# Second block: the gate projection in the last three rounds of the recurrent stage, its sigmoids from copies

## The chip, the cores and the metric

The kernel runs on one core of a Trainium2 chip. The metric is the device time of one execution in microseconds, the median of three runs. Everything is 32-bit floating point.

## The reference

Two transformer blocks run one after the other on 512 tokens of width 1024. The change is in the second. There one input projection feeds two branches, a gated delta rule (eight heads of 128, forwards and backwards over chunks of 64 tokens) and latent attention. A sigmoid gate for each branch weighs their outputs:

```python
h = rms_norm_2(x, g_mix[l]) * (1.0 + sc1) + sh1
proj = h @ w_in[l]
dn_qkv, dn_z, dn_b, dn_a, c_q, c_kv, k_r, gates = jnp.split(proj, split_at, axis=-1)
y_dn = gated_deltanet_branch(dn_qkv, dn_z, dn_b, dn_a, ...) @ w_o_dn[l]
y_mla = mla_branch(c_q, c_kv, k_r, ...) @ w_o_mla[l]
g_dn, g_mla = jnp.split(jax.nn.sigmoid(gates), N_BRANCHES, axis=-1)
merged = g_dn * y_dn + g_mla * y_mla
x = x + gt1 * (merged @ w_out[l])
```

After it come the router and sixteen experts. The part of `proj` that the change moves is `g_dn`'s, columns 4960 to 5983 of `w_in`, called `gd` in the kernel.

## The kernel before

Activations lie transposed: 128 channels on the partitions, 512 tokens along them, eight such tiles (`h3` for `h`). A projection of width 1024 is eight products j, each of eight matmuls (kk) of 128x128 weights by 128x512 into one PSUM bank. In the trace each 32-bit matmul has two records, so a projection to 1024 has 128.

The code writes out one instruction list for each engine, as Python generators. `woven` (L96) takes one step of each stream in turn, and such a step is a **slot**. `rounds` (L1244) starts 12 rounds of 32 slots. In round r the recurrent ("delta") stage runs five stages on different heads: the fetch of head r (its projections), the preparation of r-1, the scores of r-2 (the triangular inverse, many 64x64 products), the state chain of r-3, and the post stage of r-4. In a slot their order is chain, scores, post, preparation, fetch, and after these what is given as `beside`. Round 8 has no fetch left, round 9 only chain 6, scores 7 and post 5, round 10 chain 7 and post 6, round 11 post 7. Each queue is carried out in order, so a wait holds all that stands behind it.

**The chain** (`pe_dchain` L2432, `ac_dchain` L2472) has eight steps of four slots: in slot 0 products with the state, in slot 1 the one of the inverse (after ScalarE has scaled the last), in slot 2 two more (after ScalarE's copy U2), and nothing in slot 3. VectorE then updates the state for the next step. The end of the last step of head 7 is marked `dheaded 7`. **The post stage** (`pe_dpost` L2522, `ac_dpost` L2545) turns a head's output with 32 short products in slot 1 and sums squares with one 128x512 product in slot 6; ScalarE takes a logarithm and an exponential in slot 8, for heads over 4 with a table load ahead of them. `pe_dscores` (L2301) issues nothing in slots that are 3 (mod 4), but for one group in slot 3.

**The latent stage** follows (`pe_mla` L2668, `ac_mla` L2699, `sp_mla` L2644, `dv_mla` L2731). `gd` is its first projection (L2669), into banks 3 and 4, each bank emptied by a sigmoid into `ga3` (L2704). Then come cq (four products, banks 2 and 1), a wait for cq's last copy, ck (two products), kr (one), and the output projection `odn` of the delta branch. `odn` waits for all the `gd` sigmoids (L2683), since VectorE multiplies each of its products by `ga3` (L2752). After `odn`'s second product TensorE does the rotation of kr and sums the squares of cq and ck, which ScalarE has made after kr's copy, a sine and a cosine and a table load.

**Loads.** SP issues all weight loads in one order. `Ring` has five slots of 1 MB; `claim` (L272) waits for TensorE to have freed what a slot held. `sp_mla` begins with a wait for `dheaded 7` and the load of the positions; the loads of `gd` stand behind it (L2647).

Of the kernel before, what the change touches and what calls it, by code (L numbers as in the profile page):

```python
# [104 lines left out]
def run(stream):  # L105
    for _ in stream:
        pass


def chain(*streams):  # L110
    for s in streams:
        yield from s


def idle(n):
# [96 lines left out]
def program(nc, a, out):  # L212

    ctx = ExitStack()
    with ctx:
# [1028 lines left out]
        def rounds(*stages, beside={}):  # L1244

            for r in range(8 + len(stages) - 1):
                woven(*[stages[n](r - n) for n in (3, 2, 4, 1, 0) if 0 <= r - n < 8], *[beside[n]() for n in beside if n == r])
# [893 lines left out]
        def sp_dfetch(sp, hd):  # L2141
            src = [rows128(win[:, b0 + hd * 128:b0 + hd * 128 + 128]) for b0 in (0, 1024, 2048, 3072)]
            for i in range(2):
                load(sp, ("dq", hd, i), (0, (0, P), (8, 128), src[2 * i]), (1024, (0, P), (8, 128), src[2 * i + 1]))
# [441 lines left out]
        def none32(ct):  # L2586
            yield from idle(32)

        def sp_delta(sp):
            sp_gates(sp)  # L2590
            for hd in range(8):
                sp_dfetch(sp, hd)

        def pe_delta(pe):
            pe_gates(pe)
            nx = (s_dv, ndv["nx", "mix2", 0])
            left = {0: nx, 1: nx, 2: nx, 3: nx}
            rounds(lambda c: pe_dfetch(pe, c, left), lambda c: pe_dprep(pe, c, left), lambda c: pe_dscores(pe, c, left),
                   lambda c: pe_dchain(pe, c), lambda c: pe_dpost(pe, c, left))

        def ac_delta(ac):
            ac_gates(ac)
            rounds(lambda c: ac_dfetch(ac, c), lambda c: ac_dprep(ac, c), lambda c: ac_dscores(ac, c), lambda c: ac_dchain(ac, c), lambda c: ac_dpost(ac, c))

        def gp_delta(gp):
            gp_gates(gp)
# [37 lines left out]
        def sp_mla(sp):  # L2644
            sp.wait_ge(s_pe, npe["dheaded", 7])
            sp.dma(pi, a["pos"].broadcast_to([P, 512])).then_inc(s_pos, 16)
            run(sp_proj(sp, "gd", win[:, 4960:5984], KT, D))  # L2647
            run(sp_proj(sp, "cq", win[:, 4128:4640], KT, 512))
            run(sp_proj(sp, "ck", win[:, 4640:4896], KT, 256))
            k = claim(sp, ("kr",), 2)  # L2650
# [15 lines left out]


        def pe_mla(pe):  # L2668
            run(pe_proj(pe, "gd", h3, KT, D, (3, 4), lambda j: (s_ac, nac["gd", j])))  # L2669
            pe.wait_ge(s_dv, ndv["dof", 7])  # L2670
            run(pe_proj(pe, "cq", h3, KT, 512, (2, 1), lambda j: (s_ac, nac["cq", j])))
            pe.wait_ge(s_ac, nac["cq", 3])
            run(pe_proj(pe, "ck", h3, KT, 256, (2, 1), lambda j: (s_ac, nac["ck", j])))
            k, there = ring["kr",]
            v = wv(k, 0, (0, P), (8, 128))
# [4 lines left out]
            m.then_inc(s_pe, npe("kr"))  # L2680
            pe.wait_ge(s_dv, ndv["dpost", 7])
            odn = pe_proj(pe, "odn", od3, KT, D, (0, 1), lambda j: (s_dv, ndv["odn", j]))
            pe.wait_ge(s_ac, nac["gd", 7])  # L2683
            pe.wait_ge(s_ac, nac["ck", 1])
            for j, _ in enumerate(odn):
                if j == 1:
# [12 lines left out]
        def ac_mla(ac):  # L2699
            ac.wait_ge(s_pe, npe["dheaded", 7])  # L2700
            ac.wait_ge(s_dv, ndv["doo", 7, 7])
            for j in range(8):
                ac.wait_ge(s_pe, npe["pj", "gd", j])
                ac.act(ga3[:, j, :], BK[3 + j % 2][:, :], ACT.Sigmoid).then_inc(s_ac, nac("gd", j))  # L2704
            for key, src, nk, *_ in LATS:
                for j in range(nk):
                    ac.wait_ge(s_pe, npe["pj", key, j])
                    ac.act(src[:, j, :], BK[2 - j % 2][:, :], COPY).then_inc(s_ac, nac(key, j))
            ac.wait_ge(s_pe, npe["kr"])
            ac.wait_ge(s_dv, ndv["pos"])  # L2710
            ac.act(R0, BK[7][:, :], COPY).then_inc(s_ac, nac("rope", "kr"))
            ac.wait_ge(s_dv, ndv["ang"])
            ac.act(SI, ang, ACT.Sin).then_inc(s_ac, nac("sin"))
            ac.act(CO, ang, ACT.Sin, scale=0.5).then_inc(s_ac, nac("cos"))
# [893 lines left out]
```

## Time and profile before

| | us |
|---|---|
| median of three runs | 3571.12 |
| lowest, highest | 3561.42, 3572.17 |
| the profiled execution | 3565.9 |
| its span | 3564.1 |

| engine | busy us | share |
|---|---|---|
| TensorE, matmul | 3423.7 | 96% |
| TensorE, weight load | 2251.5 | 63% |
| VectorE | 1521.5 | 43% |
| ScalarE | 752.4 | 21% |
| GpSimd | 354.5 | 10% |

The times of the rows are from the start of the span. Matmuls are pipelined and their ends are modelled, so TensorE's busy time holds some overlap; the distance from one start to the next is the safer measure. "Idle before" in brackets is the time the engine stood idle ahead of the group, with what ended it. A line of the timeline merges like instructions. The rounds of the delta stage can be found by the 32 short products of the post stage (`con,A 64*128 64x64`): they start at 2322.78 for round 7, 2388.87 for round 8, 2436.34 for round 9, 2475.85 for round 10 and 2508.79 for round 11. The gate projection `gd` runs from 2516.42.

### The profile page before, as it was taken

The numbers are of one execution on the slowest core, as the hardware profiler recorded it, in microseconds if no ns is written. First come the engines' busy times: TensorE is split into PE (matmuls) and PEld (weight loads), VectorE is DVE, ScalarE is ACT, GpSimd is POOL, SyncE is SP. The second block draws the span as 40 slices with busy tenths as digits, with TensorE's granted clock in tenths as the row PEclk, the third lists the DMA queues.
The fourth block names the chain that finished last, engine by engine and source line by source line (L and its number), as shares of the span: only waits on it lengthen the run. The fifth ranks groups of instructions, "written<-read, shape, count | busy, mean of one in ns | idle before, by whom it ended". The sixth has DMA issues, their size and how long they took to land.

```text
span 3564.1 us, 56007 instructions
## 1 busy us (share of the span) xinstructions
PE 3423.7 (96%) x24870; PEld 2251.5 (63%) x24870; DVE 1521.5 (43%) x2761; ACT 752.4 (21%) x1564; POOL 354.5 (10%) x274
## 2 busy tenths in 40 slices
PE   8999998999999999999998999998999999899999
PEld 3566676888884658888885566566445656534344
DVE  4454454788743225778633444544112204201011
ACT  2323232211003035211002222233112320211111
POOL 0010110233000000122001110012000001000000
PEclk9999998999999999999999999999899999899999
DMA  5321202255641320256522101000321114599996
GB/s 195 119 73 45 85 7 84 86 174 179 207 146 48 84 71 1 60 177 198 157 73 71 48 25 37 2 2 2 103 65 42 48 43 148 241 421 421 421 421 256
DMA packets 355809, 453.12 MB, mean 127 GB/s; under 512 B 25712, under 2 KB 282992, under 8 KB 331760
## 3 DMA queue, kind: packets, MB, share of 16 engines
q1 hardware_dynamic: 355568, 449.55, 36.8%
q8 instruction: 195, 3.19, 0.4%
q14 instruction: 46, 0.38, 0.0%
HBM read 445.27 MB, written 4.20 MB: 126 GB/s over the span
## 4 chain that ended last, share of the span: by engine, by line
PE 90%; DVE 5%; ACT 3%; issue 1%; DMA 1%; SPq 0%; POOLq 0%; POOL 0%; DVEq 0%; ACTq 0%
PE bank L79 90%; DVE A L70 2%; DVE A L76 1%; ACT A L87 1%; ACT H L87 1%; PE bank L82 0%; DVE X L76 0%; DVE H L70 0%; ACT SM L87 0%; DVE SM L76 0%; DVE A L73 0%; DMA A<-in_x 0%; ACT L90 0%; ACT X L87 0%; DMA W<-in_mlp_up 0%
## 5 line engine op out<-in xcount | busy, mean ns | idle before, releaser
L79 PE MATMUL bank<-A 64*64 64x64 f32 (+4 forms) x13728 | 1078.6, 263 | 55.3 <-ACT A L87 35.1
L79 PEld LDWEIGHTS bank<-A 64*64 64x64 f32 (+2 forms) x13728 | 862.3, 150 | 295.5 <-issue 126.6
L79 PE MATMUL bank<-A,W 128*128 128x256 f32 (+1 forms) x2240 | 721.1, 476 | 3.0 <-DMA W<-in_rw_g 1.8
L79 PE MATMUL bank<-H,W 128*128 128x512 f32 (+2 forms) x1712 | 625.4, 519 | 17.0 <-ACT H L87 14.4
L79 PEld LDWEIGHTS bank<-A,W 128*128 128x128 f32 x2240 | 418.9, 191 | 254.3 <-issue 213.0
L87 ACT ACTIVATE A<-bank 128x512 f32<-128x512 f32 (+5 forms) x517 | 223.3, 435 | 1537.1 <-PE bank L79 1493.4
L79 PEld LDWEIGHTS bank<-H,W 128*128 128x128 f32 (+1 forms) x1712 | 316.6, 190 | 288.8 <-issue 258.8
L79 PE MATMUL bank<-A,H 128*64 128x512 f32 (+2 forms) x1224 | 310.5, 574 | 6.9 <-ACT H L87 6.4
L70 DVE TENSOR_TENSOR A<-bank,A 128x256 f32<-128x256 f32 (+1 forms) x350 | 157.5, 461 | 184.3 <-PE bank L79 164.3
L79 PEld LDWEIGHTS bank<-A,H 128*64 128x64 f32 (+1 forms) x1224 | 114.8, 146 | 173.1 <-issue 146.0
L70 POOL TENSOR_TENSOR A<-A 128x512 f32<-128x512 f32 (+1 forms) x103 | 146.4, 1428 | 739.0 <-ACT A L87 372.2
L87 ACT ACTIVATE A<-A 128x512 f32<-128x512 f32 (+1 forms) x230 | 133.8, 609 | 376.9 <-DVE A L70 358.4
L79 PE MATMUL bank<-W,H 128*64 128x512 f32 (+3 forms) x952 | 208.8, 475 | 4.8 <-ACT H L87 4.8
L76 DVE SCALAR_TENSOR_TENSOR SM<-W,cact,SM 128x512 f32<-128x512 f32 x206 | 184.4, 895 | 9.3
L70 DVE TENSOR_TENSOR A<-W 128x512 f32<-128x512 f32 x152 | 110.8, 770 | 177.7 <-PE bank L79 87.4
L70 DVE TENSOR_TENSOR A<-bank,SM 128x512 f32<-128x512 f32 x16 | 10.3, 686 | 392.9 <-PE bank L79 392.9
L79 PEld LDWEIGHTS bank<-W,H 128*64 128x64 f32 (+1 forms) x952 | 85.6, 159 | 104.2 <-issue 98.4
L70 POOL TENSOR_TENSOR SM<-SM 128x512 f32<-128x512 f32 x31 | 41.2, 1329 | 819.6 <-ACT SM L87 817.3
L79 PE MATMUL bank<-H,A 128*128 128x256 f32 x448 | 107.4, 381 | 0.0
L76 DVE SCALAR_TENSOR_TENSOR X<-bank,mods,X 128x256 f32<-128x256 f32 (+1 forms) x144 | 86.4, 602 | 48.5 <-PE bank L79 43.6
L79 PE MATMUL bank<-A,con 128*128 128x512 f32 (+2 forms) x174 | 91.5, 650 | 14.4 <-ACT A L87 14.4
L70 DVE TENSOR_TENSOR A<-A 128x512 f32<-128x512 f32 (+3 forms) x58 | 54.0, 940 | 102.3 <-ACT A L87 101.3
(179 smaller groups left out, 2551.1 us busy)
## 6 DMA issues: line engine op xcount, KB each, us to landing
A<-in_w_gate SPq DMA_DIRECT2D x47, 1024.0 KB, 19.3
W<-in_mod_w SPq DMA_DIRECT2D x45, 1024.0 KB, 7.3
A<-in_w_up SPq DMA_DIRECT2D x42, 1024.0 KB, 15.3
A<-in_w_down SPq DMA_DIRECT2D x35, 1024.0 KB, 25.4
W<-in_mlp_up SPq DMA_DIRECT2D x64, 512.0 KB, 5.4
W<-in_mlp_down SPq DMA_DIRECT2D x128, 256.0 KB, 4.0
W<-in_w_mod SPq DMA_DIRECT2D x24, 1024.0 KB, 5.6
W<-in_w_up SPq DMA_DIRECT2D x22, 1024.0 KB, 14.6
```

Of the source, the lines that this page charges most:

```text
L70: return self.e.tensor_tensor(o, x, y, op)
L76: return self.e.scalar_tensor_tensor(out=o, in0=x, scalar=s, in1=y, op0=op0, op1=op1, **kw)
L79: return self.e.matmul(o, l, r, start=start, stop=stop, skip_group_check=True)
L87: return self.e.activation(o, i, func, bias=bias, scale=scale)
```

## The change

`gd`'s 64 matmuls become a stream `pe_dgate` that is given to `rounds` as `beside` for rounds 9, 10 and 11, 32 steps of it in each (`take`). A product j takes nine slots: eight with one matmul each and an empty one, so it covers slots 9j to 9j+7 counted from the start of round 9, and the last matmul stands in slot 6 of round 11. All go into bank 0. In each ninth slot ScalarE copies the bank to one of eight free places `GDR`, and the next product waits for that. The four loads are issued at the end of `sp_delta`, ahead of the wait for `dheaded 7`. In the latent stage cq is now first and uses banks 3 and 4, the wait ahead of ck is on post 7's variance, and the eight sigmoids read the copies, after kr's copy and ahead of the sine.

```diff
@@ -110,6 +110,13 @@
 def chain(*streams):
     for s in streams:
         yield from s
+
+
+def take(stream, n):
+
+    for _ in range(n):
+        next(stream, None)
+        yield
 
 
 def idle(n):
@@ -2586,21 +2593,54 @@
         def none32(ct):
             yield from idle(32)
 
+
+
+        GDR = [A[:, k:k + 512] for k in (26624, 27136, 27648, 28160, 21184, 21696, 22208, 22720)]
+
+        def pe_dgate(pe):
+            pe.wait_ge(s_ac, nac["r1"])
+            for j in range(8):
+                lk = ("pj", "gd", j // 2 * 256)
+                k, there = ring[lk]
+                pe.wait_ge(ring.sems[k], there)
+                if j:
+                    pe.wait_ge(s_ac, nac["gdr", j - 1])
+                for kk in range(8):
+                    m = pe.mm(BK[0][:, :], wv(k, 0, (0, P), (8, 256))[:, kk, j % 2 * 128:j % 2 * 128 + 128], h3[:, kk, :], kk == 0, kk == 7)
+                    if kk < 7:
+                        yield
+                if j % 2:
+                    npe.mark_next("free", *lk)
+                m.then_inc(s_pe, npe("pj", "gd", j))
+                yield
+                yield
+
+        def ac_dgate(ac):
+            for j in range(8):
+                yield from idle(8)
+                ac.wait_ge(s_pe, npe["pj", "gd", j])
+                ac.act(GDR[j], BK[0][:, :], COPY).then_inc(s_ac, nac("gdr", j))
+                yield
+
+        def with_gate(gate):
+            return {r: lambda: take(gate, 32) for r in (9, 10, 11)}
+
         def sp_delta(sp):
             sp_gates(sp)
             for hd in range(8):
                 sp_dfetch(sp, hd)
+            run(sp_proj(sp, "gd", win[:, 4960:5984], KT, D))
 
         def pe_delta(pe):
             pe_gates(pe)
             nx = (s_dv, ndv["nx", "mix2", 0])
             left = {0: nx, 1: nx, 2: nx, 3: nx}
             rounds(lambda c: pe_dfetch(pe, c, left), lambda c: pe_dprep(pe, c, left), lambda c: pe_dscores(pe, c, left),
-                   lambda c: pe_dchain(pe, c), lambda c: pe_dpost(pe, c, left))
+                   lambda c: pe_dchain(pe, c), lambda c: pe_dpost(pe, c, left), beside=with_gate(pe_dgate(pe)))
 
         def ac_delta(ac):
             ac_gates(ac)
-            rounds(lambda c: ac_dfetch(ac, c), lambda c: ac_dprep(ac, c), lambda c: ac_dscores(ac, c), lambda c: ac_dchain(ac, c), lambda c: ac_dpost(ac, c))
+            rounds(lambda c: ac_dfetch(ac, c), lambda c: ac_dprep(ac, c), lambda c: ac_dscores(ac, c), lambda c: ac_dchain(ac, c), lambda c: ac_dpost(ac, c), beside=with_gate(ac_dgate(ac)))
 
         def gp_delta(gp):
             gp_gates(gp)
@@ -2644,7 +2684,6 @@
         def sp_mla(sp):
             sp.wait_ge(s_pe, npe["dheaded", 7])
             sp.dma(pi, a["pos"].broadcast_to([P, 512])).then_inc(s_pos, 16)
-            run(sp_proj(sp, "gd", win[:, 4960:5984], KT, D))
             run(sp_proj(sp, "cq", win[:, 4128:4640], KT, 512))
             run(sp_proj(sp, "ck", win[:, 4640:4896], KT, 256))
             k = claim(sp, ("kr",), 2)
@@ -2666,10 +2705,8 @@
 
 
         def pe_mla(pe):
-            run(pe_proj(pe, "gd", h3, KT, D, (3, 4), lambda j: (s_ac, nac["gd", j])))
-            pe.wait_ge(s_dv, ndv["dof", 7])
-            run(pe_proj(pe, "cq", h3, KT, 512, (2, 1), lambda j: (s_ac, nac["cq", j])))
-            pe.wait_ge(s_ac, nac["cq", 3])
+            run(pe_proj(pe, "cq", h3, KT, 512, (3, 4), lambda j: (s_ac, nac["cq", j])))
+            pe.wait_ge(s_dv, ndv["dov", 7])
             run(pe_proj(pe, "ck", h3, KT, 256, (2, 1), lambda j: (s_ac, nac["ck", j])))
             k, there = ring["kr",]
             v = wv(k, 0, (0, P), (8, 128))
@@ -2680,7 +2717,7 @@
             m.then_inc(s_pe, npe("kr"))
             pe.wait_ge(s_dv, ndv["dpost", 7])
             odn = pe_proj(pe, "odn", od3, KT, D, (0, 1), lambda j: (s_dv, ndv["odn", j]))
-            pe.wait_ge(s_ac, nac["gd", 7])
+
             pe.wait_ge(s_ac, nac["ck", 1])
             for j, _ in enumerate(odn):
                 if j == 1:
@@ -2699,16 +2736,16 @@
         def ac_mla(ac):
             ac.wait_ge(s_pe, npe["dheaded", 7])
             ac.wait_ge(s_dv, ndv["doo", 7, 7])
-            for j in range(8):
-                ac.wait_ge(s_pe, npe["pj", "gd", j])
-                ac.act(ga3[:, j, :], BK[3 + j % 2][:, :], ACT.Sigmoid).then_inc(s_ac, nac("gd", j))
             for key, src, nk, *_ in LATS:
                 for j in range(nk):
                     ac.wait_ge(s_pe, npe["pj", key, j])
-                    ac.act(src[:, j, :], BK[2 - j % 2][:, :], COPY).then_inc(s_ac, nac(key, j))
+                    ac.act(src[:, j, :], BK[3 + j % 2 if key == "cq" else 2 - j % 2][:, :], COPY).then_inc(s_ac, nac(key, j))
             ac.wait_ge(s_pe, npe["kr"])
             ac.wait_ge(s_dv, ndv["pos"])
             ac.act(R0, BK[7][:, :], COPY).then_inc(s_ac, nac("rope", "kr"))
+            for j in range(8):
+                ac.wait_ge(s_ac, nac["gdr", j])
+                ac.act(ga3[:, j, :], GDR[j], ACT.Sigmoid).then_inc(s_ac, nac("gd", j))
             ac.wait_ge(s_dv, ndv["ang"])
             ac.act(SI, ang, ACT.Sin).then_inc(s_ac, nac("sin"))
             ac.act(CO, ang, ACT.Sin, scale=0.5).then_inc(s_ac, nac("cos"))
```

## Rows read from the trace of the kernel before

**Rows 1.** The page: TensorE's busy time and share, and its granted clock by slices.

```profile
PE 3423.7 (96%) x24870; PEld 2251.5 (63%) x24870; DVE 1521.5 (43%) x2761; ACT 752.4 (21%) x1564; POOL 354.5 (10%) x274
PEclk9999998999999999999999999999899999899999
```

**Rows 2.** The page: the chain that ended last, by engine.

```profile
PE 90%; DVE 5%; ACT 3%; issue 1%; DMA 1%; SPq 0%; POOLq 0%; POOL 0%; DVEq 0%; ACTq 0%
```

**Rows 3.** By stretch: length, busy of PE, PEld, DVE, ACT, POOL, PEclk, DMA, GB/s.

```profile
2322.78:2388.87 66.09, 64.73 (x822) 41.49 (x821) 33.45 (x69) 19.78 (x40) 5.67 (x5) 1.00 0.01 2
2436.34:2475.85 39.51, 34.63 (x728) 28.84 (x726) 19.45 (x47) 11.93 (x27) 25.38 (x18) 1.00 0.01 2
2475.85:2508.79 32.94, 23.53 (x179) 13.82 (x179) 11.05 (x33) 8.22 (x20) 0.00 (x0) 0.65 0.00 1
2508.79:2516.42 7.63, 5.55 (x35) 4.18 (x36) 0.69 (x1) 1.23 (x2) 0.00 (x0) 0.50 0.91 251
2516.42:2573.29 56.87, 56.87 (x130) 25.15 (x130) 6.31 (x11) 8.01 (x11) 0.00 (x0) 0.97 0.37 110
```

**Rows 4.** By stretch, within round 10, the same columns.

```profile
2485.00:2490.00 5.00, 2.88 (x20) 1.83 (x20) 2.50 (x6) 1.76 (x4) 0.00 (x0) 0.58 0.00 0
```

**Rows 5.** Timeline of PE, rounds 7 and 9: start, us, what, count.

```profile
2352.12 4.83 PE L79 MATMUL bank<-A 64*64 64x128 f32 x116
...
2361.38 4.83 PE L79 MATMUL bank<-A 64*64 64x128 f32 x116
...
2455.03 4.83 PE L79 MATMUL bank<-A 64*64 64x128 f32 x116 [0.52 <-DVE A L76]
...
2460.66 4.83 PE L79 MATMUL bank<-A 64*64 64x128 f32 x116
```

**Rows 6.** Timeline of PE, round 8: a lone 128x512 product and the next group.

```profile
2392.38 1.12 PE L79 MATMUL bank<-A,con 128*128 128x512 f32 x2
2393.43 0.66 PE L79 MATMUL bank<-A 128*64 128x128 f32 x8
```

**Rows 7.** Timeline of PE, round 7: chain groups with no wait, and the turn.

```profile
2322.41 0.44 PE L79 MATMUL bank<-A 64*64 64x128 f32 x4
2322.78 2.00 PE L79 MATMUL bank<-con,A 64*128 64x64 f32 x32
2324.61 0.81 PE L79 MATMUL bank<-A 64*128 64x128 f32 x8
2325.26 1.10 PE L79 MATMUL bank<-con,A 64*64 64x64 f32 x32
```

**Rows 8.** Timeline of PE, round 10: groups behind a wait.

```profile
2486.47 2.63 PE L79 MATMUL bank<-A 64*128 64x128 f32 x16 [2.24 <-ACT A L87]
2489.66 0.69 PE L79 MATMUL bank<-A 64*64 64x128 f32 x4 [0.56 <-ACT A L87]
```

**Rows 9.** Timeline of PE: the last sum of squares, and the first ck product.

```profile
2514.55 2.08 PE L79 MATMUL bank<-A,con 128*128 128x512 f32 x2 [2.08 <-ACT A L87]
...
2601.44 18.72 PE L79 MATMUL bank<-H,W 128*128 128x512 f32 x43 [0.69 <-ACT A L87]
```

**Rows 10.** Timeline of ACT: table load, last gate eviction, the sines, the squares.

```profile
2483.67 1.28 ACT L90 ACT_TABLE_LOAD   x1
...
2573.33 0.60 ACT L87 ACTIVATE A<-bank 128x512 f32<-128x512 f32 x1 [6.27 <-PE bank L79]
...
2624.26 1.15 ACT L87 ACTIVATE A<-A 128x512 f32<-128x512 f32 x2
...
2626.72 3.23 ACT L87 ACTIVATE SM<-A 128x512 f32<-128x512 f32 x6
```

**Rows 11.** Timeline of PE: the sums of cq's and ck's squares.

```profile
2636.98 5.42 PE L79 MATMUL bank<-SM,con 128*128 128x512 f32 x12
```

**Rows 12.** Timeline of SP and PEld: the first gate load and its use.

```profile
2508.82 51.76 SPq L93 DMA_DIRECT2D W<-in_w_in  x9
...
2516.23 0.52 PEld L79 LDWEIGHTS bank<-H,W 128*128 128x128 f32 x2 [1.19 <-DMA W<-in_w_in]
```

## The prediction

> **What bounds the kernel now.** I read four views in this order. The page's busy shares and its chain of waits come first: TensorE is busy 96% of the span [rows 1], and 90% of the chain that ended last is its matmuls [rows 2]. So what counts is how long TensorE's queue is, and where it waits. The granted clock comes second: it is mostly at its full level, 2.4 GHz, and dips in a few slices [rows 1]. Third comes busy time by stretch, cut at the start of each head's 32 small "turn" products (the first step of the post stage), which stands in slot 1 of each round [rows 3]. A full round (round 7, all five stages) takes 66.09 us, of which 64.73 busy. Round 9 takes 39.51 us with 34.63 busy, and round 10 takes 32.94 us with 23.53 busy at a mean granted clock of 0.65. The 7.63 us after the last turn are at 0.50, and then the gate projection and its 128 records run, 56.87 us to the next product. Fourth is the timeline inside round 10: each step of the state chain is two or three short groups of products, each behind a wait for ScalarE or VectorE, and the clock falls to its half level, 1.2 GHz, from about 2486 us [rows 4, 8]. These holes are what the change can use. Holes in rounds 9 and 10 and after the last turn are 4.9, 9.4 and 2.1 us; what the low clock costs there comes on top.
>
> **What a product costs when it is moved.** Back to back, one 128x512 matmul takes 0.86 us: ScalarE evicts a gate product of eight each 6.27 + 0.60 = 6.87 us, the eighth at 2573.33 [rows 10], and 56.87 us cover all eight with a slow start [rows 3]. A matmul has two records. Alone between short products it costs more: the one at 2392.38 is followed by the next product at 2393.43, 1.05 us [rows 6]. The extra 0.19 us is there once for each uninterrupted group, as four fetch products show: round 7 repeats its pattern in 9.26 us (2352.12 to 2361.38), round 9 the same 132 records without the four in 5.63 us (2455.03 to 2460.66), so four cost 3.63 us, which is 0.19 + 4 x 0.86 [rows 5]. That round 7 and round 9 differ by just the products, with nothing absorbed, is also what tells me that round 9's busy time is real: 64.73 - 34.63 = 30.1 us for 28 fetch products (25.4 us), three of the preparation (3.2 us), and 32 short records that fall on the other side of the cut [rows 3].
>
> The 64 matmuls go one to a slot, with every ninth slot empty. In slots that are 3 (mod 4) the chain and the scores issue nothing, so there the product follows another one directly and costs 0.86. Counted slot by slot: one in round 9 before the turn (1.05 us), 22 alone and 7 adjacent in the stretch of round 9 (29.1 us), 21 and 7 in that of round 10 (28.1 us), and six after the last turn.
>
> **Round 9:** 34.63 busy + 29.1 + waits left over. A full round with 28 such products keeps 66.09 - 64.73 = 1.4 us of waits. I take 2.0, because ScalarE's logarithm, with a table load of 1.28 us ahead of it [rows 10], stands in slot 8 of this round and the first product's eviction copy is queued behind it: 65.7 us.
>
> **Round 10** at full clock: a chain step is 0.37 to 0.44 for its first group, 0.65 to 0.81 for the second [rows 7] and up to 0.66 for the third [rows 6], so 1.7 to 1.9, eight of them 14.4 us; the turn is 1.83 (2322.78 to 2324.61) [rows 7] and the sum-of-squares product 1.05. With 28.1 us of gate products that is 45.4. The waits of a step (0.56 at 2489.66, and some 0.4 for its other groups) [rows 8] are shorter than the product now put into each; what stays are the three empty slots, and the wait of 2.24 us behind ScalarE's table load and logarithm [rows 8], of which 1.05 are covered. I take 2.3 us for these: 47.7 us.
>
> **After the last turn:** the turn at full clock 1.83; then five gate products, the sum of squares and one more, 0.19 + 7 x 0.86 = 6.2 us. The wait of 2.08 ahead of the sum of squares [rows 9] lies under the five. 8.0 us.
>
> **The sum.** Before, from round 9's turn to the first latent-query (cq) product: 39.51 + 32.94 + 7.63 + 56.87 = 136.95 us [rows 3]. After: 1.05 + 65.7 + 47.7 + 8.0 = 122.45. Gain 14.5 us.
>
> **The rest of the change.** The wait for cq's last eviction ahead of the first ck product, 0.69 us [rows 9], goes, since cq now uses banks 3 and 4, and the wait put there is on the last variance, long done by then: +0.7 us. The bounds: nothing to 0.9.
> The eight eviction copies are 0.60 us each on ScalarE [rows 10], which is busy 11.9 us of round 9's 39.5. Behind a waiting copy are queued the chain's own copies; but the copy stands last in its slot and waits for a product TensorE issued a slot earlier, so it can hold TensorE only where the next gate product needs the one bank. That is at most eight times 0.6 us, mostly inside the empty slot. I count 0 beyond the waits above, with 4 us as upper bound.
> The sigmoids (eight of some 0.57 us, as the two sines in 1.15 [rows 10]; four to five us) with their table load of 1.28 move into the path kr copy - sine - squares - latent sums. That delays the squares by 5.9 us: they ended at 2626.72 + 3.23 = 2629.95 [rows 10], and TensorE needs them at 2636.98 [rows 11]. Cover 7.0 us, so 0; if the cover were gone, up to 5.9.
> On SP the four gate loads move ahead of the wait for the last head and of the position load. SP then stands in no one's way, for their slots come free in rounds 5 to 7 and DMA is at 0.01 there; 0. The first cq load takes the place of the first gate load: issued 2508.82, usable 2516.23, with 1.19 us of waiting [rows 12]. It is now needed some 10 us after the chain's last product and lands after about 8, so this wait goes too (it is inside the 7.63). What is late next is nothing on this path but TensorE itself.
> All together 15.2 us. The profiled execution, 3565.9 us with a span of 3564.1, would be 3550.7. It lies 5 us under the median of the three runs shown, 3571.1; from that median, 3555.9. I predict 3556.
>
> **A rule of the skill.** The rows say 1.05 for a lone product and 0.86 in a row. The Trainium skill ("TensorE: Matmul & The Clock Gate", Part 2, on LDWEIGHTS) says that the queue can pull a weight load ahead of a running matmul where the rows of the array don't conflict or the load goes to the background buffer. By that rule a lone product would cost 0.86 like the others, and the gain would be 24 us in place of 15. The trace does not agree in this mix: 1.05 us at 2392.38. Another rule, "Perfetto Trace Analysis", "Identifying the Most-Contended Engine", judges TensorE by weight loads, not matmul busy time. By it round 9, with loads busy 28.84 of 39.51 us, would have room; the comparison of rounds 7 and 9 speaks against it.
>
> **Rivals.**
> (1) Part of the product's cost is absorbed. 45 products pay 0.19 for standing alone, so with none paying it the gain is 15.2 + 8.6 = 24 us: 3547. For it: the loads busy 28.84 us of round 9 [rows 3]. Against: both row comparisons above. 0.12.
> (2) Slot-by-slot coupling costs more. The one bank, with its copy behind the chain's work on ScalarE, leaves the boundary of each product open by up to 0.6 (4 us) and round 9 keeps all of its 4.9 us of holes instead of 2.0 (3 us more). The gain is then 15.2 - 7 = 8 us: 3563. For it: ScalarE's order is fixed, and one bank has no second to go on with. Against: the copy has an empty slot. 0.23.
> (3) Slower: the granted clock stays at half through round 10 and to the first cq product, as it was there before [rows 3, 4]. Everything in those stretches doubles but the waits, +48 - 2: the time becomes 3556 + 46 = 3602. The price of the clock passes the gain where it holds the half level for a third of that. Against: the full rounds, with the same mix of short and long products, kept 1.00 [rows 3]. For it: in round 10 the scores' products are gone, and the short ones are mostly waits. 0.05, this and smaller slowdowns.
> (4) The gain is real but comes to little, since the expert weights' stream at the end gives it back. Its first load waits for this path's own results, so it should shift along with it. 0.05, gain 0 to 8, about 3567.
>
> **How the numbers follow.** My case has 0.55, a gain of 11 to 19 us. A measurement of this kernel can tell about 0.3%, 11 us, from no change. Faster by more than that: my case with most of its band (0.53), rival 1 (0.12) and a small part of rival 2 (0.03): 0.68. Within: 0.26. Slower: 0.06. The range takes in rival 1 with the lower of the runs, and most of rival 2: 3544 to 3568.
>
> **What would show each step.** In the new profile: turn to turn, rounds 9 and 10 at 65.7 and 47.7 us; 8 us from the last turn to cq; a granted clock of 1.00 from 2440 us to there; lone gate products spaced 1.05; no wait ahead of the first ck product; squares done before the rope product. If round 9 stays under 62 us, rival 1 is right; if waits for ScalarE at the gate's first records add up to several us, rival 2; if round 10 is beyond 60 us with a clock under 0.8, rival 3. Wrong also if the late stages don't keep their lengths.

## The result, and the profile after

The changed kernel takes 3544.66 us, the median of four runs (3540.89 to 3549.41), where the kernel before takes 3568.78. The ratio is 0.9932, with a 95% interval from 0.9918 to 0.9946: faster by 24 us, 19 to 29. Run twice more on other occasions it gave 0.9934 (0.9920 to 0.9947) and 0.9944 (0.9930 to 0.9958). Over all 16 executions of it and the 68 of the kernel before that ran beside it or beside its variants the means are 3546.1 and 3568.1 us, 22.0 apart. I had 15.2, and 3556 for the time. The profiled execution took 3549.4 us, its span 3547.6; that is 16.5 less than the span of the one the sum was made against. The 16.5 lies close to the sum, in part by chance, as shown below; what lies beyond the sum is the subject of much of what follows.

The page of the changed kernel, busy times, granted clock by slices, and the chain that ended last:

```profile
PE 3419.5 (96%) x24870; PEld 2240.6 (63%) x24870; DVE 1523.9 (43%) x2761; ACT 756.1 (21%) x1572; POOL 354.5 (10%) x274
PEclk9999998999999999999999999999999999899999
PE 90%; DVE 5%; ACT 3%; DMA 1%; issue 1%; SPq 0%; POOLq 0%; POOL 0%; DVEq 0%; ACTq 0%
```

TensorE has as many records as before and still carries 90% of the chain [rows 1, 2]. What changed shows by stretches, cut at the same places as [rows 3]: the turns that open rounds 9, 10 and 11, and the first cq product (columns as there). All times in rows are us from the start of the span.

```profile
2439.81:2506.45 66.64, 64.44 (x786) 39.60 (x785) 20.16 (x46) 13.50 (x29) 24.68 (x18) 0.97 0.01 2
2506.45:2552.53 46.08, 43.87 (x237) 19.11 (x235) 10.95 (x33) 10.51 (x24) 0.00 (x0) 1.00 0.02 6
2552.53:2560.58 8.05, 8.05 (x48) 4.63 (x48) 1.35 (x2) 1.23 (x2) 0.00 (x0) 1.00 1.01 325
```

Round 10 had 23.53 us of work in 32.94 and a clock of 0.65; now it has 43.87 in 46.08 at 1.00. After the last turn there isn't a hole left. The 56.87 us of the gate projection have no stretch any more. Together 120.8 us, plus 1.05 for the one matmul ahead of the first turn, against 136.95. The clock of 0.97 in round 9 belongs to one place: behind the longest wait, 1.63 us, a group of 72 records takes 4.25 us, and 2.72 in other places of the round.

```profile
2460.41 1.12 PE L79 MATMUL bank<-H,W 128*128 128x512 f32 x2 [1.63 <-ACT A L87]
2461.46 4.25 PE L79 MATMUL bank<-A 64*128 64x128 f32 x72
```

The timeline of TensorE in round 10, the piece with the largest waits:

```profile
2518.73 1.12 PE L79 MATMUL bank<-H,W 128*128 128x512 f32 x2
2519.78 0.43 PE L79 MATMUL bank<-A 64*64 64x128 f32 x4
2520.15 1.13 PE L79 MATMUL bank<-H,W 128*128 128x512 f32 x2
2522.03 0.86 PE L79 MATMUL bank<-A 64*128 64x128 f32 x8 [0.76 <-ACT A L87]
2522.82 1.98 PE L79 MATMUL bank<-H,W 128*128 128x512 f32 x4
2524.73 0.66 PE L79 MATMUL bank<-A 128*64 128x128 f32 x8
2525.95 0.44 PE L79 MATMUL bank<-A 64*64 64x128 f32 x4 [0.56 <-ACT A L87]
2526.34 1.12 PE L79 MATMUL bank<-H,W 128*128 128x512 f32 x2
```

A lone gate matmul (`H,W`, x2) is followed after 1.05 us (2518.73 to 2519.78), a pair of adjacent ones after 1.91 (2522.82 to 2524.73). The wait of 0.56 that stood in each of these chain steps of the kernel before (one is in [rows 8]) is there only where a slot is empty, here at 2525.95. The wait behind the table load is 0.76 where it was 2.24 [rows 8].

ScalarE in the latent stage, the counterpart of [rows 10], and TensorE's sums of squares, of [rows 11]:

```profile
2608.84 0.60 ACT L87 ACTIVATE A<-bank 128x512 f32<-128x512 f32 x1 [6.27 <-PE bank L79]
2609.45 1.28 ACT L87 ACT_TABLE_LOAD   x1
2610.75 4.26 ACT L87 ACTIVATE A<-A 128x512 f32<-128x512 f32 x8
2615.03 1.28 ACT L87 ACT_TABLE_LOAD   x1
2616.33 1.15 ACT L87 ACTIVATE A<-A 128x512 f32<-128x512 f32 x2
2617.49 1.28 ACT L90 ACT_TABLE_LOAD   x1
2618.79 3.23 ACT L87 ACTIVATE SM<-A 128x512 f32<-128x512 f32 x6
```

```profile
2559.72 49.09 PE L79 MATMUL bank<-H,W 128*128 128x512 f32 x114
...
2622.47 1.08 PE L79 MATMUL bank<-A,con 64*64 64x512 f32 x4
2623.47 5.42 PE L79 MATMUL bank<-SM,con 128*128 128x512 f32 x12
```

The eight sigmoids take 4.26 us, the squares end at 2622.02, and TensorE wants them at 2623.47: covered, with 1.4 us to spare. Through cq, ck and kr TensorE has no wait.

### The profile page after: what moved, and what is told of

Its sections match the earlier page's. It is cut to its first block, busy times and chain, and to the rows that moved or that the text cites. A ratio compares the mean times of both kernels' runs of the same rounds, so it can differ in the third digit from the quotient of the medians.

```text
span 3547.6 us, 56015 instructions
## 1 busy us (share of the span) xinstructions
PE 3419.5 (96%) x24870; PEld 2240.6 (63%) x24870; DVE 1523.9 (43%) x2761; ACT 756.1 (21%) x1572; POOL 354.5 (10%) x274
## 4 chain that ended last, share of the span: by engine, by line
PE 90%; DVE 5%; ACT 3%; DMA 1%; issue 1%; SPq 0%; POOLq 0%; POOL 0%; DVEq 0%; ACTq 0%
PE bank L79 90%; DVE A L70 1%; DVE A L76 1%; ACT A L87 1%; ACT H L87 1%; PE bank L82 0%; DVE X L76 0%; DVE H L70 0%; ACT SM L87 0%; DVE SM L76 0%; DVE A L73 0%; DMA A<-in_x 0%; ACT L90 0%; ACT X L87 0%; DMA W<-in_mlp_up 0%
## 5 line engine op out<-in xcount | busy, mean ns | idle before, releaser
L79 PE MATMUL bank<-H,W 128*128 128x512 f32 (+2 forms) x1712 | 638.4, 522 | 18.5 <-ACT H L87 14.4
L79 PEld LDWEIGHTS bank<-H,A 128*128 128x128 f32 x448 | 84.2, 190 | 12.4 <-DVE H L73 0.8
## 6 DMA issues: line engine op xcount, KB each, us to landing
A<-in_w_up SPq DMA_DIRECT2D x42, 1024.0 KB, 15.2
W<-in_w_up SPq DMA_DIRECT2D x22, 1024.0 KB, 14.5
```

What stands on the lines that cost most here:

```text
L79: return self.e.matmul(o, l, r, start=start, stop=stop, skip_group_check=True)
```

## The experiments

**The two kernels again.** They ask how much of the 24 us is the change and how much the execution that happened to be profiled.

> The kernel before, unchanged. Local theory (the gain is the holes and the low clock of rounds 9 to 11, 15 to 17 us, and the rest of the 24 us between the medians is the spread of executions): ratio 1.000 within 0.2%, executions spread over some 10 us, and the longer ones have a lower granted clock. Downstream theory (the later stages are really shorter in the changed kernel): executions of this kernel lie close together near 3568.

Measured: 3568.17 us, median of 12 (3561.11 to 3573.90), ratio 1.0003 (0.9992 to 1.0014). The spread is as the local theory has it, and its faster executions have a mean granted clock of 0.978, its slowest of 0.973. But the profile shows something that I hadn't counted on. In this execution round 9's turn comes 4 us earlier than in [rows 3], and the gate projection begins at the same time, 2516.27:

```profile
2432.34:2471.86 39.52, 34.64 (x729) 28.84 (x727) 19.46 (x47) 11.94 (x27) 25.37 (x18) 1.00 0.01 2
2471.86:2508.65 36.79, 27.60 (x179) 16.33 (x179) 11.25 (x33) 8.21 (x20) 0.00 (x0) 0.55 0.00 1
2508.65:2516.27 7.62, 5.54 (x34) 4.23 (x35) 0.69 (x1) 1.23 (x2) 0.00 (x0) 0.50 0.84 261
```

Round 10 takes 36.79 us in place of 32.94, at a mean clock of 0.55 in place of 0.65. So round 10 of the kernel before has two lengths, and my sum was made against the shorter. The longer one has come with an earlier arrival both times that it was seen (here and in `shift` below), so that the gate projection begins between 2516.26 and 2516.83 in all four profiles that have the old rounds.

> The changed kernel, unchanged. Local theory: 15 to 19 us below the kernel before in the same rounds (ratio 0.9947 to 0.9958), with the stages behind the first ck product as long as before. Downstream theory: 24 us again (0.9932), some 8 of them behind the first ck product.

> The changed kernel once more, beside the aligned version on the same chip. From the executions so far: 3544 to 3546, ratio 0.993 to 0.9945. Turn of round 9 to the first cq product 119 to 121 us, at a granted clock of 1.00 in round 10. Rival to the reading that the low clock is gone for good there: an execution in which round 10 falls to half again, and 130 us or more.

Measured: 3544.39 us (0.9920 to 0.9947), and 3548.69 us (0.9930 to 0.9958). The first lies on the downstream theory's 0.9932, with the local theory's 0.9947 at the end of its interval; the second is 3 us above the times that I expected, and its ratio holds by a hair. The size alone doesn't decide; the table below, of the part behind the first sum of squares, does. The rounds agree to a hundredth between these two executions. This is the third one:

```profile
2443.80:2508.92 65.12, 62.92 (x787) 38.17 (x785) 20.13 (x46) 13.49 (x29) 24.68 (x18) 1.00 0.01 2
2508.92:2554.99 46.07, 43.87 (x236) 19.10 (x234) 10.94 (x33) 10.50 (x24) 0.00 (x0) 1.00 0.01 4
2554.99:2563.04 8.05, 8.05 (x48) 4.63 (x47) 1.35 (x2) 1.23 (x2) 0.00 (x0) 1.00 1.04 332
```

119.24 us, and 119.23 in the second. In the first profile it was 120.77, since round 9 had a clock of 0.97. In none of the three profiles of the changed kernel was round 10 below 1.00.

**A pure shift.** The kernel before, without the last two of the eight gate products.

```diff
-            run(sp_proj(sp, "gd", win[:, 4960:5984], KT, D))
+            run(sp_proj(sp, "gd", win[:, 4960:5728], KT, 768))
...
-            run(pe_proj(pe, "gd", h3, KT, D, (3, 4), lambda j: (s_ac, nac["gd", j])))
+            run(pe_proj(pe, "gd", h3, KT, 768, (3, 4), lambda j: (s_ac, nac["gd", j])))
...
-                ac.wait_ge(s_pe, npe["pj", "gd", j])
+                ac.wait_ge(s_pe, npe["pj", "gd", min(j, 5)])
```

> The kernel before with only six of the eight gate products (the last two sigmoids read the banks of the products before them); the rounds are untouched. It removes 2 x 6.87 = 13.7 us from the latent stage and makes all that is later start 13.7 us earlier. Local theory: 13.7 us faster within 2 us, 3555. Downstream theory, by which an earlier start makes later stages shorter: 19 to 23 us faster, 3546 to 3550.

Measured: 3551.45 us, ratio 0.9957 (0.9943 to 0.9970), 15 us faster, 11 to 20. The local theory has 13.7 in the interval; the downstream theory, with 19 to 23, has only its lower end in it. Its profile has the long form of round 10 again:

```profile
2472.41:2509.20 36.79, 27.60 (x178) 16.34 (x178) 11.26 (x33) 8.21 (x20) 0.00 (x0) 0.55 0.00 1
```

From the first sum of squares to the end of the span, the code of all these kernels is the same. The table takes the start of that row and the span of each profile:

| kernel | first sum of squares | span | between |
|---|---|---|---|
| before | 2636.98 | 3564.1 | 927.1 |
| before_again | 2636.95 | 3562.6 | 925.7 |
| edges | 2635.88 | 3561.7 | 925.8 |
| shift | 2623.79 | 3549.5 | 925.7 |
| keepwarm | 2640.52 | 3566.2 | 925.7 |
| after | 2623.47 | 3547.6 | 924.1 |
| after_again | 2617.54 | 3541.9 | 924.4 |
| after_third | 2625.94 | 3550.0 | 924.1 |
| mixed | 2620.28 | 3544.3 | 924.0 |
| early_table | 2612.47 | 3539.6 | 927.1 |
| mixed_early | 2613.83 | 3537.7 | 923.9 |
| late | 2620.56 | 3547.6 | 927.0 |
| aligned | 2606.85 | 3534.0 | 927.2 |
| aligned_again | 2616.71 | 3543.8 | 927.1 |

(The versions from `mixed` on are described below.) `shift` reaches this part 13.2 us earlier than `before_again` and takes as long in it, 925.7 us: an earlier start alone shortens nothing. The changed kernel is 1.3 to 3 us shorter there. `late`, `early_table` and `aligned`, which have the change's code from there on, are as long as the longest, and `mixed` and `mixed_early` as short as the shortest. So this isn't what the change does to the later work. It goes with the granted clock: in the 50 us that begin 300 us behind the first sum of squares it is 0.94 in all five profiles of 927 us, 1.00 in three of the five of about 924 (`after`, `mixed`, `mixed_early`), and 0.97 in the other six. What sets it there is open. The time of arrival alone does not: `late` (2620.56) and `mixed` (2620.28) arrive within 0.3 us of each other and differ by 3 us.

**The two small parts alone.**

```diff
             for hd in range(8):
                 sp_dfetch(sp, hd)
+            run(sp_proj(sp, "gd", win[:, 4960:5984], KT, D))
...
-            run(sp_proj(sp, "gd", win[:, 4960:5984], KT, D))
...
-            pe.wait_ge(s_ac, nac["cq", 3])
-            run(pe_proj(pe, "ck", h3, KT, 256, (2, 1), lambda j: (s_ac, nac["ck", j])))
+            pe.wait_ge(s_ac, nac["gd", 7])
+            run(pe_proj(pe, "ck", h3, KT, 256, (3, 4), lambda j: (s_ac, nac["ck", j])))
...
-                    ac.act(src[:, j, :], BK[2 - j % 2][:, :], COPY).then_inc(s_ac, nac(key, j))
+                    ac.act(src[:, j, :], BK[2 - j % 2 if key == "cq" else 3 + j % 2][:, :], COPY).then_inc(s_ac, nac(key, j))
```

> The kernel before with the two small parts alone: the four gate loads are issued at the end of the recurrent stage, and ck's products go to banks 3 and 4, with no wait for cq's last copy. My sum: the 1.2 us wait for the first gate load goes and then nothing is late (a further 0.5 us of clock), and 0.7 us at the first ck product: 1.9 to 2.4 us faster, 3566.5 where the kernel before has 3568.8. Rival (another late thing takes the place of the load): 0.7 us. Read from the profile, since the spread of executions is larger.

Measured: 3564.02 us, ratio 0.9994 (0.9984 to 1.0004), not to be told from no change; the profile is needed. In it the stretch behind the last turn is as long as in [rows 3], though there is no load to wait for:

```profile
2508.64:2516.26 7.62, 5.54 (x34) 4.32 (x35) 0.69 (x1) 1.23 (x2) 0.00 (x0) 0.50 0.56 172
```

The load wait of 1.19 us [rows 12] was one of the weight-load path, under the matmul of 2.08 us at half clock [rows 9]. It cost nothing, and the 1.2 to 1.7 us that I had expected from its going didn't come. The round 8 turn comes 0.15 us earlier than in the kernel before (2388.72, 2388.87) and the first sum of squares 1.10 earlier (2635.88, 2636.98): 0.95 us is the gain at ck, where I had 0.7 and a bound of 0.9.

**Only the clock.**

```diff
+        def pe_warm(pe, n):
+            for _ in range(n):
+                pe.wait_ge(s_ac, nac["r1"])
+                pe.mm(BK[0][:, 0:128], C("ones"), C("ident"), True, True).then_inc(s_pe, npe())
+                yield
...
-                   lambda c: pe_dchain(pe, c), lambda c: pe_dpost(pe, c, left))
+                   lambda c: pe_dchain(pe, c), lambda c: pe_dpost(pe, c, left), beside={10: lambda: pe_warm(pe, 32), 11: lambda: pe_warm(pe, 6)})
```

> The kernel before with one short product of 128 columns (its result is thrown away) in each slot of round 10 and in six slots of round 11, and nothing moved. It adds 38 x some 0.4 us of work, most of it inside the waits. It prices the clock by itself. My theory (the low level there is the answer to TensorE's idleness): the clock stays at 1.00, round 10 turn to turn takes 30 to 32 us in place of 32.9, the stretch to the first gate record 5.5 to 6.5 in place of 7.6, the first gate product 6.9 in place of 8.8: 4 to 6 us faster in all, 3561 to 3563 where the kernel before has 3566.5. Rival (the holes, not the clock, were what the moved products used): the clock stays low and the fillers cost: 0 to 8 us slower.

Measured: 3571.06 us, ratio 1.0000 (0.9990 to 1.0010). The total is the rival's; the parts are mixed. These are the stretches of round 10 and of what follows its end, and one of four chain steps inside round 10:

```profile
2476.14:2512.39 36.25, 33.58 (x244) 23.38 (x242) 11.05 (x33) 8.34 (x20) 0.00 (x0) 0.81 0.00 1
2512.39:2519.93 7.54, 4.44 (x45) 3.35 (x44) 1.38 (x2) 2.79 (x4) 0.00 (x0) 1.00 0.82 246
2495.93:2509.73 13.80, 13.24 (x115) 9.01 (x113) 4.69 (x18) 2.58 (x8) 0.00 (x0) 1.00 0.00 1
```

```profile
2475.32 0.49 PE L79 MATMUL bank<-con 128*128 128x128 f32 x2
...
2476.14 3.68 PE L79 MATMUL bank<-con,A 64*128 64x64 f32 x32
...
2493.92 0.86 PE L79 MATMUL bank<-A 64*128 64x128 f32 x8 [1.82 <-ACT A L87]
...
2516.47 1.13 PE L79 MATMUL bank<-A,con 128*128 128x512 f32 x2 [0.77 <-ACT A L87]
2519.93 10.55 PE L79 MATMUL bank<-H,W 128*128 128x512 f32 x20 [2.33 <-DMA W<-in_w_in]
```

Once the clock is at 1.00 a chain step takes 3.45 us with its fillers (13.80 / 4), where it took 4.25 at half (from 2489.66 [rows 8] the next groups of its kind in the kernel before start at 2493.91 and 2498.16). But the clock fell at the turn: it took 3.68 us, as long as the one at half clock (2508.79 in the kernel before), where the kernel before needs 2.00 for it at 2475.85, and it stayed at half until about 2489, so the round took 36.25 us. Only one filler had run by then (2475.32). So this run doesn't say whether fillers in round 9 would have held the clock; it says that those in round 10 didn't keep it from half over the next 12 us, although TensorE had no wait there. Behind the last turn the clock was full, and the work ended sooner. What came next was the load: TensorE waited 2.33 us for it, and the gate projection began at 2519.93. Behind that wait the clock fell once more (0.75 over the next 6.87 us), and the first gate product took 8.87 us from there to its copy, as in the kernel before (8.84), where I had expected 6.9. So the faster clock of half a round brought nothing here: the fillers cost work of their own, and the load that cost nothing in the kernel before was the next in line. In the change the loads must be early in any case, since the moved products run ahead of the last head's end. Why the clock fell is open.

**Which round.** The gate products two matmuls to a slot, five slots a product, in rounds 10 and 11 only:

```diff
...
-            return {r: lambda: take(gate, 32) for r in (9, 10, 11)}
+            return {r: lambda: take(gate, 32) for r in (10, 11)}
...
                     if kk < 7:
-                        yield
+                        if kk % 2:
+                            yield
...
-                yield from idle(8)
+                yield from idle(4)
```

> The changed kernel, with the gate products two matmuls to a slot (five slots a product, the last empty) in rounds 10 and 11 only; round 9 is left as in the kernel before. It tells the part of round 9 from that of rounds 10 and 11. My price: round 9 turn to turn 39.5, round 10 some 68, from the last turn to cq some 14, so 122 in all where the changed kernel had 119 to 121: 0 to 3 us slower than the changed kernel, 3545 to 3548, and the clock at 1.00 through round 10. So nearly all of the gain would be there without round 9, whose holes are few. Rival (round 9's holes carry a real part): 5 us or more slower than the changed kernel.

Measured: 3550.51 us, ratio 0.9955 (0.9940 to 0.9969); in the profile, with one pair of gate matmuls inside the first stretch:

```profile
2436.45:2477.78 41.33, 36.62 (x732) 29.49 (x731) 19.45 (x47) 11.81 (x26) 25.36 (x18) 1.00 0.01 2
2477.78:2545.23 67.45, 64.19 (x285) 28.43 (x283) 10.94 (x33) 11.36 (x26) 0.00 (x0) 1.00 0.06 15
2545.23:2557.66 12.43, 11.74 (x55) 6.07 (x55) 1.38 (x2) 1.71 (x3) 0.00 (x0) 1.00 0.83 237
```

121.2 us where I expected 122, beside 120.3 (with the matmul ahead of the turn) in the changed kernel. Moving part of the work into round 9 is worth about 1 us; the gain is made in rounds 10 and 11. The comparison isn't clean, for its pairs form 23 groups where the changed kernel has 45 matmuls that pay for standing alone; by the price that is an estimated 4 us in favour of `late`. The changed kernel's own rows point the same way, however: in round 9 thirty matmuls took 65.12 - 39.51 + 1.05 = 26.66 us, 0.89 each, which is what they cost in the old projection (56.87 / 64). The other 34 took 13.55 us there (46.07 + 8.05 against 32.94 + 7.63), where the projection needed 30.2. The median is 3550.5 where I expected 3545 to 3548, and differs from those of the changed kernel by more (3544.4 and 3548.7); in the profiles 2.6 to 2.9 us of that is the part behind the first sum of squares, of which the table says that it belongs to no edit.

**The price of a lone matmul.** The first four products in groups of four every fourth slot of round 9, the others as in the change:

```diff
...
                     if kk < 7:
-                        yield
+                        if j >= 4:
+                            yield
+                        elif kk == 3:
+                            yield from idle(4)
...
-                yield
-                yield
+                yield from idle(4 if j < 4 else 2)
...
-                yield from idle(8)
+                yield from idle(5 if j < 4 else 8)
...
-                yield
+                yield from idle(3 if j < 4 else 1)
```

> The changed kernel, with the first four gate products issued as groups of four matmuls every fourth slot of round 9 and the others one to a slot as before. By my price (0.19 us for each uninterrupted group, 0.86 for a matmul) round 9 takes in 32 matmuls for 29.0 us in place of 29 for 29.1, and three fewer are left for the rounds behind it: 2 to 3 us faster than the changed kernel, if round 9's waits don't grow. Rival (a lone product costs nothing extra, its 0.19 is time that would be waited anyway): no change, or up to 2 us slower because holes in three of four slots stay open.

Measured: 3546.06 us, ratio 0.9935 (0.9921 to 0.9949), no faster than the changed kernel, where I expected 2 to 3 us less. The profile separates two effects:

```profile
2439.17:2501.56 62.39, 61.03 (x786) 39.09 (x784) 18.85 (x46) 13.99 (x30) 22.03 (x16) 1.00 0.01 2
2501.56:2551.29 49.73, 46.23 (x238) 20.07 (x236) 10.96 (x33) 9.91 (x23) 0.00 (x0) 0.97 0.02 5
```

```profile
2518.09 1.12 PE L79 MATMUL bank<-H,W 128*128 128x512 f32 x2 [2.56 <-ACT A L87]
...
2520.18 3.38 PE L79 MATMUL bank<-H,W 128*128 128x512 f32 x4
```

Round 9 has 29 gate matmuls in this stretch, as in the changed kernel, with seven groups of four and one alone. By the price that is 26.5 us in place of 29.1. It took 62.39 us in place of 65.12, so 2.7 less where 2.6 were due: the 0.19 us is real, and a matmul pays it once for each uninterrupted group. The rest gave it back. A whole group, 3.63 us, now stands ahead of the first turn in place of one matmul, 1.05. Round 10 holds one matmul more, and the copy of a finished product now falls on slot 8, where ScalarE's table load and logarithm stand. The next product's first matmul then waits 2.56 us, and behind the wait the clock is at half for a moment: the two matmuls at 2520.18 take 3.38 us in place of 1.98. From round 9 to cq it is 121.8 us, with the group ahead of the turn, beside 120.3.

**The table load.**

```diff
-            yield from idle(4)
-            ac.wait_ge(s_dv, ndv["dov", hd])
+            yield
             if hd > 4:
                 ac.ln_exp()
+            yield from idle(3)
+            ac.wait_ge(s_dv, ndv["dov", hd])
```

> The changed kernel, with the table load of ScalarE's post stage moved from slot 8 to slot 5 of its round, for the heads that have one. The stall ahead of U2's copy in rounds 9 and 10 (1.6 and 0.8 us of TensorE's waits in the changed kernel) should lose up to 1.28 us each: 1.5 to 2 us faster than the changed kernel. Rival (the load then holds a copy of slot 6 or 7): no change.

> Both edits of the two kernels above together: the groups of four in round 9, and the early table load. My sum: 3 to 5 us faster than the changed kernel, 3540 to 3541. Where a group of four already covers the stall, the table load gives only round 10's 0.8 us.

Measured: 3546.20 us (0.9914 to 0.9943), and with both edits 3542.00 us (0.9907 to 0.9938). Rounds 9 and 10 of the first, and round 10 of the second:

```profile
2432.59:2496.27 63.68, 62.91 (x786) 38.16 (x784) 20.50 (x46) 13.39 (x29) 25.02 (x18) 1.00 0.01 2
2496.27:2541.52 45.25, 43.80 (x236) 19.11 (x234) 10.97 (x33) 10.40 (x24) 0.00 (x0) 1.00 0.02 5
```

```profile
2498.18:2544.85 46.67, 44.60 (x239) 19.50 (x237) 10.97 (x33) 9.80 (x23) 0.00 (x0) 1.00 0.03 6
```

63.68 and 45.25 where the changed kernel has 65.12 and 46.07: 2.3 us off the two waits, as expected or a little more. In the whole time the first doesn't show, for the interval is wider than 2 us. Together the two edits save 3.1 us in round 10 against `mixed` (46.67 to 49.73), so the stall was what `mixed` suffered from: 1.4 us of it in waits and 1.6 in busy time, the moment at half clock behind the stall. From round 9 to cq, with what stands ahead of the first turn, the first version takes 118.0 us and the second 118.8, beside 120.3: the second saves 1.5 us where I expected 3 to 5, and is by its stretches no better than the early table load alone.

**All of it.** Groups of four in round 9 from slot 4 on, the early table load, and in round 10 one matmul in slots 0 and 1 of a chain step, two in slot 2, none in slot 3:

```diff
...
                     if kk < 7:
-                        yield
+                        h = 2 * j + kk // 4
+                        if h < 7:
+                            if kk % 4 == 3:
+                                yield from idle(4)
+                        elif kk % 4 < 2:
+                            yield
+                        elif kk % 4 == 3:
+                            yield
+                            yield
...
```

> The changed kernel with all that the runs so far point to: groups of four in round 9, early table load, and in round 10 one matmul in slots 0 and 1 of a chain step, two in slot 2 and none in slot 3, so that the end of a product always falls on the slot in which the chain issues nothing, and never on a hole. Round 9 turn to turn some 61, round 10 some 45, the tail 6 to 7 us: 117 in all or slightly less, where the changed kernel had 119 to 121: 3 to 4 us faster than the changed kernel, 3540 to 3542, 0.9925 of the kernel before. Rival (the copy of each second step then opens a hole of 0.3 to 0.5 us, and the stall behind the logarithm stays): as fast as the kernel with both edits, 3542 to 3543.

> The aligned version once more, beside the changed kernel. By the stretch from the end of round 8 to the latent stage, 187.1 us where the changed kernel had 190.1: 3 us faster than the changed kernel in the same rounds, which an interval of 0.13% can hardly tell; if the medians stand within 1 us, the gain is in the profile alone and stays unproved in the time.

Measured: 3545.43 us (0.9916 to 0.9948), and 3542.98 us (0.9912 to 0.9942) beside 3548.69 of the changed kernel on the same chip. Both profiles agree to 0.01 us; this is the second:

```profile
2436.51:2498.72 62.21, 60.99 (x787) 39.09 (x785) 19.55 (x47) 13.39 (x29) 24.92 (x18) 1.00 0.01 2
2498.72:2546.87 48.15, 47.57 (x245) 20.44 (x243) 10.96 (x33) 10.62 (x24) 0.00 (x0) 1.00 0.03 5
2546.87:2553.81 6.94, 5.73 (x41) 3.41 (x41) 0.69 (x1) 2.71 (x4) 0.00 (x0) 1.00 1.04 333
```

117.30 us, and nothing ahead of the first turn, beside 120.3: 3.0 us less, as forecast in all, though round 10 took 48.15 us, with four matmuls more than in the changed kernel, where I had written some 45. 2.3 of the 3.0 the early table load gives alone. Over both occasions the means are 3543.5 (12 executions) and 3546.1 (16), 2.7 apart with an interval that just reaches zero. On the chip where both ran side by side they are 3542.8 and 3548.4, six executions each: 5.6 apart, 2 to 9. So the total too says faster there; its size is taken from the stretches.

## Why the prediction was right, and where it was not

**The products' price held.** 1.05 us alone and 0.86 in a row, read from single rows [rows 5, 6], came back in the changed kernel's own rows, and `mixed` confirmed the difference, 2.7 us for 2.6. The Trainium skill's rule of the weight load pulled ahead ("TensorE: Matmul & The Clock Gate", Part 2), and with it rival 1's mechanism, has no support between groups of different kinds: the first weight load of the pair at 2522.82 begins with the pair, and its next ones, at 2523.35 and 2523.78, under a running matmul. That the 0.19 us is this first load is likely; no run changes the load alone. The Trainium skill's other rule, on weight loads (beside the share of peak arithmetic) as a better measure of room than matmul busy time ("Perfetto Trace Analysis", "Identifying the Most-Contended Engine"), would have promised room in round 9, whose load share was 28.84 of 39.51 us. The rows give 0.89 us for each matmul moved there, as much as it had cost in the old projection.

**The three stretches.** Forecast 65.7, 47.7 and 8.0 us. Measured 66.64, 46.08 and 8.05 in the first profile, and 65.12, 46.07 and 8.05 in the third. The sum with the matmul ahead of the turn was 122.45 and came out at 121.8 and 120.3. In round 10 I had kept 2.3 us of waits and 14.4 us for the chain's groups; the new waits were 2.2 (46.08 less 43.87), so what I took too long, by 1.6 us, is the chain's groups. I counted eight whole steps; the stretch holds seven and a lone short group, 12.7 us by the distances from start to start.

**The step that was mis-sized** is the length of the old round 10. The sum subtracts from one execution, and I took its 32.94 us as the kernel's own. Two of four profiles with the old rounds have 36.79, at a clock of 0.55. With 138.9 us as the mean of the two forms (136.95 and 140.8, the latter 83.93 of `before_again`'s stretches and 56.87) and 120.8 as the mean of the changed kernel's three profiles, the rounds and the gate give 18.1 us where I had 14.5. ck gives 0.95 where I had 0.7. That makes 19 us of the change's own, beside 22.0 between the means; the other 3 us stay open. Two more differences stand in the profiles, and neither is an effect of the edits. The part behind the first sum of squares was shorter by 926.4 - 924.2 = 2.2 us. And the changed kernel's three profiles reached the turn of round 8, up to which TensorE has the same work, 4.3 us later (2391.1 on the mean, beside 2386.8 of `before` and `before_again`). With these two the parts come to 17.0, and the spans of the same profiles differ by 16.9 (3563.4 and 3546.5). The 16.5 between the first two spans was made up in the same way: 15.1 us in the stretches and 0.8 from cq to the sums of squares, less 2.4 of later arrival, and 3.0 behind the first sum of squares. What I read correctly as "what the low clock costs comes on top" I had priced from one sample of something that varies.

**The time was right by luck in part.** The forecast was 3556 and the median is 3544.66, 0.7 us inside the lower end of the range. That end was set for rival 1; my own case's gain of 11 to 19 us does not hold the 24 of the medians, nor the 22.0 of the means. Of the 11.3 us that the time was off, 2.3 are the base, for I started from a median of 3571.1 and four executions give 3568.8; 8.9 are gain that the sum did not have. So the mechanism was my case's, and the total came out at rival 1's (3547), by other causes than rival 1's.

**Nothing for the moved pieces.** The sigmoids' delay was covered, with 1.4 us left (forecast 1.1). The eviction copies held TensorE in a few places only; its waits from round 9 to cq sum to 4.4 us in two stretches (66.64 - 64.44 and 46.08 - 43.87), forecast 4.3. The first cq load was hidden. That the load's wait would go "too" was an empty gain, as `edges` shows, and the sum rightly had no term for it. `keepwarm` shows that the load is the next to be waited for once the work ahead of it ends sooner.

**The rivals.** Rival 2 (coupling) would have given 3563; its stall exists, and `mixed` shows it at 2.56 us where a product's copy falls on slot 8, but in the change no copy falls there in round 10; one does in round 9, where `early_table` took 1.4 us off. Rival 3 (the clock stays low) didn't occur in any of the three profiles; `mixed` alone was below 1.00 in round 10, at 0.97. Rival 4 was wrong: the stream of expert weights started 12.8 us earlier in the changed kernel's first profile (2976.85, before 2989.62), about what the stages before it had gained (13.5), and no profile gave anything back.

## What to carry to other kernels

Independent work is worth most where a dependent chain leaves the matmul engine in short waits and at its low clock: here 120 us replaced 137 to 141, nearly all of the gain made in the two rounds that had little else to do, and about 1 us in the round that was already full. Price a moved matmul in the place it goes to, and let the end of each accumulation, with its copy and its single bank, fall where neither the chain nor a table load stands. Take the length of a stretch at a low clock from several executions, since it is the term that varies.

## What the runs showed of the hardware that I had not expected

Arriving 4 us earlier at round 10 brought the kernel before nothing: the granted clock fell earlier, the round took 36.79 us in place of 32.94, and the gate projection started at 2516.27 in place of 2516.42. That the earlier arrival is the cause is not shown; the two have come together in two profiles of two. In `keepwarm` the clock fell at the start of round 10, where in the kernel before it fell at about 2486, and was back at 1.00 from about 2490 on (mean 0.81 over the round), where in the kernel before it stayed at half. And a weight-load wait of 1.19 us ahead of a matmul can cost nothing at all, when the matmul before it is still running at half clock.
